# Six MLP tiles of the third token block moved to the two stretches around the last block's output projection

## The reference

```python
h = modulate(rmsnorm(x, norm_mix_w[l]), shift_a, scale_a)
proj = (h @ w_in[l]).astype(f32)
mixed = token_mix(proj, ...)          # 4 retention heads and 4 gated DeltaNet heads
x = x + gate_a[:, None, :] * (mixed @ w_out[l])
h = modulate(rmsnorm(x, norm_mlp_w[l]), shift_m, scale_m)
x = x + gate_m[:, None, :] * (jnp.square(jax.nn.relu(h @ w_ff1[l])) @ w_ff2[l])
...
return rmsnorm(x, norm_final_w)
```

## Time and profile before

| What | us |
|---|---|
| median of 3 runs | 3048.26 |
| the profiled execution, whole time | 3046.6 |
| its span in the trace | 3044.8 |
| last FF2 tile of unit 15 ends, first OUT matmul starts | 2603.85, 2617.13 |
| last OUT matmul ends, FF1 of block 3 starts | 2662.2, 2674.42 |

### The profile page before, as it was taken

One profiled execution on the slowest core, in us unless ns is written; L12 is line 12 of the kernel. 1 busy time (PEld: TensorE's weight loads), 2 busy tenths in 40 slices (PEclk: granted clock), 3 DMA queues, 4 the chain that ended last, 5 costly groups with the idle time before them and its releaser, 6 DMA issues.

```text
span 3044.8 us, 37926 instructions
## 1 busy us (share of the span) xinstructions
PE 2850.4 (94%) x14376; PEld 2380.5 (78%) x14376; DVE 1324.1 (43%) x1864; ACT 1172.8 (39%) x2040; POOL 1728.8 (57%) x1324
## 2 busy tenths in 40 slices
PE   1799979999999999999999999999999999889998
PEld 1588767888888788888888788887888888668886
DVE  4555655353535335553434525545343432421123
ACT  2133443353444434353343433444333333343332
POOL 2254555575656656576555665657565655566554
PEclk9889999999999999999999999999999999999999
DMA  5521322222232323422233222422222222423332
GB/s 221 228 80 56 101 67 68 82 80 81 81 116 90 101 70 103 140 73 93 74 104 104 90 87 87 143 78 86 79 87 80 80 82 92 142 76 97 97 97 84
DMA packets 86581, 295.10 MB, mean 97 GB/s; under 512 B 10240, under 2 KB 10240, under 8 KB 82304
## 3 DMA queue, kind: packets, MB, share of 16 engines
q1 hardware_dynamic: 64944, 247.05, 25.6%
q10 hardware_dynamic: 21456, 45.62, 4.5%
HBM read 276.90 MB, written 15.73 MB: 96 GB/s over the span
## 4 chain that ended last, share of the span: by engine, by line
PE 83%; DVE 6%; POOL 5%; issue 2%; DMA 2%; ACT 2%; SPq 0%; ACTq 0%; POOLq 0%; DVEq 0%
PE acc L392 23%; PE acc L394 22%; PE acc L393 22%; PE pm L426 7%; PE pm L431 3%; DMA mixing<-in_ada_w 2%; POOL w L1388 1%; DVE mixing L1018 1%; POOL mT L1397 1%; ACT io L636 1%; PE pm L408 1%; PE pm L545 1%; DVE x L1257 1%; PE pm L518 1%; DVE io L934 1%
## 5 line engine op out<-in xcount | busy, mean ns | idle before, releaser
L1388 POOL TENSOR_TENSOR w<-raw,w 128x512 fp32r<-128x512 f32 x832 | 1116.4, 1344 | 1047.3 <-ACT w L610 1019.1
L610 ACT ACTIVATE w<-raw 128x512 fp32r<-128x512 f32 x832 | 521.0, 627 | 783.2 <-PE acc L394 662.3
L392 PE MATMUL acc<-mT,w 128*128 128x512 f32 x1280 | 517.3, 404 | 13.0 <-POOL mT L1397 5.8
L394 PE MATMUL acc<-mT,w 128*128 128x512 f32 x1280 | 501.6, 392 | 0.0
L393 PE MATMUL acc<-mT,w 128*128 128x512 f32 x1280 | 500.4, 391 | 0.0
L392 PE MATMUL acc<-hT,w 128*128 128x512 f32 x1024 | 437.1, 427 | 41.4 <-POOL w L1388 30.8
L394 PE MATMUL acc<-hT,w 128*128 128x512 f32 x1024 | 407.8, 398 | 0.0
L393 PE MATMUL acc<-hT,w 128*128 128x512 f32 x1024 | 406.7, 397 | 0.0
L1229 DVE SCALAR_TENSOR_TENSOR x<-acc,ab,x 128x512 f32<-128x512 f32 x256 | 191.4, 750 | 450.3 <-PE acc L394 450.1
L392 PE MATMUL acc<-hid,w 128*128 128x512 f32 x896 | 364.4, 407 | 13.8 <-POOL hid L1402 8.3
L394 PE MATMUL acc<-hid,w 128*128 128x512 f32 x896 | 350.3, 391 | 0.0
(11 more groups left out here) (201 smaller groups left out, 3828.0 us busy)
## 6 DMA issues: line engine op xcount, KB each, us to landing
raw<-in_w_all SPq DMA_DIRECT2D x416, 512.0 KB, 3.6
mixing<-in_ada_w SPq DMA_DIRECT2D x24, 1024.0 KB, 7.3
xr<-in_xT ACTq DMA_DIRECT2D x48, 256.0 KB, 2.9
out<-io ACTq DMA_DIRECT2D x32, 256.0 KB, 2.6
mixed_kept<-mixing ACTq DMA_DIRECT2D x28, 256.0 KB, 2.0
xr<-mixed_kept ACTq DMA_DIRECT2D x28, 256.0 KB, 2.7
x<-in_xT ACTq DMA_DIRECT2D x6, 1024.0 KB, 7.3
x<-in_xT SPq DMA_DIRECT2D x1, 2048.0 KB, 17.4
```

Source lines behind the costliest of these rows:

```text
L392: e.matmul(bank, whi, x[:, 0, :], start=first, stop=False)
L394: m = e.matmul(bank, wlo, x[:, 0, :], start=False, stop=last)
L610: e.activation(w2[:, 0, local % HALVES, :], raw[:, tile % NRAW, local % 2 * NT:(local % 2 + 1) * NT], ACT.Copy).then_inc(S["w_hi"], 1)
L1388: e.tensor_tensor(w2[:, 1, local % HALVES, :], raw[:, tile % NRAW, local % 2 * NT:(local % 2 + 1) * NT], w2[:, 0, local % HALVES, :].bitca ...
```

## The change

`dense_plan` moves six tiles and adds none. Of the 24 tiles of unit 15, the last six of block 2's MLP are held back: FF2 tiles 2 and 3 of group 6, and all four FF2 tiles of group 7. The first two stand in slots 0 to 7 of stretch 16 (2 k-steps a slot), the other four in slots 30 to 39 (3 a slot, 5 in the last). Unit 15 keeps 18 tiles: 5 k-steps in each two slots up to slot 51, 1 a slot in slots 52 to 61, 2 in the last two. In it FF1 of groups 6 and 7 now stand in a row, before FF2 of group 6.

Since block 2's residual is now complete only at slot 39, block 3 gets its own, `x1_late`, over `mixing` next to `hid_late`. ACT issues its load at slot 47 of unit 15. The hidden tile of group 7 of block 2 is kept in `hT`, free by then. The final norm of block 2 moves from slots 1 to 9 to slots 41 to 50: its squares (line 629) and their sums (929), which stood beside the readouts of group 7, now stand in slots 41 and 42 as a block, and column sums, power, diagonal, row, output tiles and output DMAs in slots 44 to 50.

```diff
             new += list(two[NG - 2]) + list(two[NG - 1])
-            per = [0] * 8 + [3] * 21 + [1] + [0] * 10 + [22] * 23 + [6]
+            held = ff(b - 2, NG - 2)[1][2:4] + ff(b - 2, NG - 1)[1]
+            new = held[0:2] + new[0:KT] + held[2:6] + new[KT:]
+            per = [2] * 8 + [3] * 21 + [1] + [3] * 9 + [5] + [22] * 23 + [6]
         elif u == 0:
             o = [(OUT, b - 1, j, 0) for j in range(KT)]
...
-                new = a5 + c5 + a6 + c6 + a7 + c7
-                per = [3] * SLOTS
-        assert sum(per) == KT * len(new), n
+                new = a5 + c5 + a6 + a7 + c6[0:2]
+                per = [3, 2] * 26 + [1] * 10 + [2] * 2
+        assert sum(per) == KT * len(new) and len(per) == SLOTS, n
...
+        last_residual = nc.sbuf_tensor("x1_late", [P, KT, NT], F32)
+        x1_late = last_residual.__enter__()
         late_hidden = nc.sbuf_tensor("hid_late", [P, 2, FFG, NT], F32R)
         hid_late = late_hidden.__enter__()
         late_hidden.__exit__(None, None, None)
+        last_residual.__exit__(None, None, None)
         mixing = sb("mixing", [P, 16, NT])
...
         def hidden(b, g):
+            if b == NB - 2 and g == NG - 1:
+                return hT[:, :, 0:FFG, :]
             return hid_late if b == NB - 1 and g % 2 else hid
+
+        def residual(b):
+            return x1_late if b == NB - 1 else x1
 
...
-                        if s == 3:
+                        if s == (44 if n == UNITS else 3):
                             column_sums(NORM["f", b - 2], bC)
-                        if s == 5:
+                        if s == (46 if n == UNITS else 5):
                             row_everywhere(NORM["f", b - 2], bC)
...
                 elif i == 0 and b == NB - 1 and g == 0:
-                    e.wait_ge(S["w_used"], used((FF2, b - 1, NG - 1, FFG - 1)))
+                    e.wait_ge(S["w_used"], used((FF2, b - 1, NG - 2, FFG - 1)))
+                elif i == 0 and b == NB - 2 and g == NG - 1:
+                    e.wait_ge(S["w_used"], used((PROJ, UNITS - 1, UNIT - 1, 0)))
                 elif i == 0 and b < NB - 1 and (b or g):
...
-                    square(NORM["m", b], i, x1[:, i, :])
-                if k % 4 == 3 and kind == FF2 and i == NG - 1:
+                    square(NORM["m", b], i, residual(b)[:, i, :])
+                if k % 4 == 3 and kind == FF2 and i == NG - 1 and b != NB - 2:
                     o = 2 * y + k // 4
                     e.wait_ge(S["ff2_evac"], 2 * NG * FFG * b + 2 * FFG * i + o + 1)
-                    square(NORM["f", b], o, x1[:, o, :])
...
+                    if n == UNITS and s in (41, 42):
+                        if s == 41:
+                            e.wait_ge(S["ff2_evac"], 2 * NG * FFG * (NB - 1))
+                        for j in range(4 * (s - 41), 4 * (s - 40)):
+                            square(NORM["f", b - 2], j, x1[:, j, :])
+                    put = s - 41 if n == UNITS else s
+                    if u == 0 and b >= 2 and put in (7, 8, 9):
+                        for j in {7: (0, 1, 2, 3), 8: (4, 5), 9: (6, 7)}[put]:
                             e.wait_ge(S["o_ready"], KT * (b - 2) + j + 1)
                             e.dma_start(out[b - 2, :, j, :], io[:, j % 4, :]).then_inc(OSEM[j % 4], 16)
-                            if j == 3:
+                            if j == 3 and n < UNITS:
                                 e.dma_start(x1[:, 0:4, :], xT[b - 1, :, 0:4, :]).then_inc(S["x1_lo_in"], 16)
-                            if j == 7:
+                            if j == 7 and n < UNITS:
                                 e.dma_start(x1[:, 4:8, :], xT[b - 1, :, 4:8, :]).then_inc(S["x1_hi_in"], 16)
+                    if n == UNITS - 1 and s == 47:
+                        e.wait_ge(S["y_out"], (LEVELS - 1) * UNITS)
+                        e.wait_ge(S["u_next"], UNITS)
+                        e.wait_ge(S["mr_kept"], 16 * UNITS)
+                        e.dma_start(x1_late[:, 0:4, :], xT[NB - 1, :, 0:4, :]).then_inc(S["x1_lo_in"], 16)
+                        e.dma_start(x1_late[:, 4:8, :], xT[NB - 1, :, 4:8, :]).then_inc(S["x1_hi_in"], 16)
                     if u == 0 and b >= 1 and 36 <= s <= 39:
                         for j in (2 * (s - 36), 2 * (s - 36) + 1):
...
+                    if n == UNITS and 41 <= s < 43:
+                        for j in range(max(1, 4 * (s - 41)), 4 * (s - 40)):
+                            add_square(NORM["f", b - 2], j)
                     if u == 0 and b >= 2:
                         f = NORM["f", b - 2]
-                        if s == 1:
+                        at = s - 41 if n == UNITS else s
+                        if at == 1 and n < UNITS:
                             add_square(f, KT - 1)
-                        if s == 3:
+                        if at == 3:
                             scaled_sums(f, bC)
-                        if s == 4:
+                        if at == 4:
                             diagonal(f)
-                        if s == 5:
+                        if at == 5:
                             keep_row(f, bC)
-                        if s in (6, 7):
-                            for j in (0, 1) if s == 6 else (2, 3):
+                        if at in (6, 7):
+                            for j in (0, 1) if at == 6 else (2, 3):
                                 out_tile(b - 2, j)
                     if n < UNITS:
                         mix(n, s)
...
-                    if u == 0 and b >= 2 and s == 4:
+                    if u == 0 and b >= 2 and s == (45 if n == UNITS else 4):
                         rms_power(NORM["f", b - 2])
```

23 lines of the change are left out of this document (11 added, 12 removed).

## The result

The changed kernel takes **3026.5 us** (median of 4 runs, 3025.48 to 3031.15). The kernel before took 3048.99 beside it (4 runs, 3047.57 to 3050.59). The ratio is 0.9935, with a 95% interval of 0.9923 to 0.9946. Forecast were 3024.9, with a range of 3018.9 to 3034. The profiled execution took 3025.81, its span is 3024.0, 20.8 less than before.

A forecast was written before the change was run, and what follows sets the result against it. PE, busy 94% of the span, bounds the kernel; only its waits and half clock can be won. Gains 12.3 + 11.9 + 2.7, less 0.5, 1.0 and 2.0, give 23.4: 3048.26 to 3024.9 us, range 3018.9 to 3034.

The forecast's parts named there:

- First stretch: Slots 0 to 7, before OUT: two held tiles cover the tail and the final norm leaves; gain 12.3 us.
- so the transpose in slot 7 waits for nothing: Slot 7: the tail with a readout ahead and one inside takes 7.5 us, against 10.9 of held tiles.
- Second stretch: Slots 30 to 39, OUT to FF1: four held tiles cover the norm; gain 11.9 us, less 0.5 for clock.
- The bound on the other side: Slots 30 to 39: all 8 high and low halves lengthen the chain by 15.8; gain 6.0 instead of 11.9.
- Rival 1: FF1 after slots 30 to 39: PE waits for low parts, POOL being shared with weights; 3030.3 us; rivals 1 to 3 together 0.29.
- Unit 15: Unit 15: two of three waits for the hidden tile gone, gain 2.7 us; thinning costs 1.0.
- rival 2: Thinned end of unit 15: the recurrence bounds it, costing 5.5 instead of 1.0; 3029.4 us; rivals 1 to 3 together 0.29.
- Final norm in the MLP: Slots 41 to 50: the norm among MLP tiles costs 2.0 us, ends 0.5 and 6.2; narrow place slot 42.
- The upper end of 6.2: Slot 42: each of DVE's four adds held for a whole POOL instruction of 1.30; total 3029.1 us.
- Rival 3: OUT: the stall only moves, loads and weights come late, first stretch brings half (6.1); 3031.0 us; rivals 1 to 3 together 0.29.
- Rival 4: Slots 30 to 50: the woven norm stalls PE up to seven times, 6.6 us each; 3068 us, slower; chance 0.04.
- Rival 5: Whole kernel: nothing measurable, the end moves by under 6 us, four stalls cost 26.4; 3048 us; chance 0.05.

The follow-up runs named there:

- thin: The changed kernel with unit 15 thinned further: 3 k-steps a slot to slot 41, 1 in slots 42 to 59, none in 60 to 63; 3030.55 us.
- two held: The changed kernel with only the first stretch filled, by two FF2 tiles of group 7; unit 15 keeps 22 tiles; 3033.32 us.
- the second run of after: The changed kernel, unaltered, measured once more; 3027.72 us.
- no hidden wait: The changed kernel with FF1 of group 6 also ahead of FF2 of group 5, hidden tiles of groups 6 and 7 sharing `hT`; 3021.96 us.
- square on ACT: The changed kernel with one four-element product moved from DVE to ACT as a square, in all 16 units; 3026.05 us.
- four held: The changed kernel with only the second stretch filled, by all four FF2 tiles of group 7; unit 15 keeps 20 tiles; 3035.8 us.
- adds early: The changed kernel with squares and adds of block 2's final norm one slot earlier, in slots 40 and 41; 3024.15 us.
- norm early: The changed kernel with block 3's MLP norm three slots earlier in stretch 16; 3023.34 us.
- no held tiles: The changed kernel with its buffer and late final norm, but all 24 tiles back in unit 15 in the old order; 3046.66 us.

## Why the prediction was right, and where its steps were off

**First stretch: 12.3 forecast, 11.4 measured.** The tail with the readout ahead of it took 8.05 us for 7.5. It held one readout inside, as was assumed, but the sum had no term for POOL, whose instructions held it up by some 1.7. The step "so the transpose in slot 7 waits for nothing" is true by its words and missed the wait: it looked at the transpose, and not at the readout that stands behind the tail on DVE. PE waits 0.73 us for that one. In other kernels it is 0.7 to 3.3.

**Second stretch: 11.9 less 0.5 forecast, 11.7 measured,** or 11.0 with the 0.7 us of half clock that reach into the second FF1 tile. The eighth k-step of FF1 started 31.8 us behind OUT's end, where 32.2 were worked out. That is near by some luck, since the sum is not what its text says: it adds 1.3 and 0.7, where the two high halves and the one low half that it names come to 2.6. The bound on the other side does not follow either: 15.8 in place of those 2.0 would leave no gain at all (1.9 lost), not one of 6.0. The waits for the low parts were 0.25, 0.22, 1.51 and 0.18, together 2.2 instead of some 3.5:

```profile
2653.34 0.47 PE L402 MATMUL acc<-mT,w 128*128 128x512 f32 x1 [0.25 <-POOL mT L1425]
...
2656.98 0.50 PE L402 MATMUL acc<-mT,w 128*128 128x512 f32 x1 [1.51 <-POOL mT L1425]
...
2658.23 0.79 PE L402 MATMUL acc<-mT,w 128*128 128x512 f32 x1 [0.18 <-POOL mT L1425]
2658.82 0.63 PE L403 MATMUL acc<-mT,w 128*128 128x512 f32 x1
```

The clock fell once behind them, as was allowed for. Rival 1 fell: it wanted 6.0 here. The crowding costs these 2.2 us and the half clock, and the norm three slots ahead took most of them away (one wait of 0.62 is left, and one of 0.47 in the held tiles).

**Unit 15: 2.7 less 1.0 forecast, 0.7 measured.** The sum is near by two errors. The recurrence cost nothing (1.0 assumed; 0.62 in the thinner kernel), so that rival 2 falls and the earlier trace rows were no measure for a unit without a next one. The gain of 2.7 shrank, since the third wait grew by 0.26 us and eight matmuls at the half clock (1.6 us) came behind it. The step that took "two of three waits gone" as their sum left out that the third one stands in a thinner unit: the half tiles on both sides of it changed.

**Final norm in the MLP: 2.0 forecast, 2.9 measured** beyond its own work. The place and the chain were right: the add began 2.6 us behind the last FF1 sum, where 2.7 were worked out. The four adds took 4.03 us; the text had 2.7 alone and 5.0 beside POOL. The wait was 2.08, in the forecast 1.0 to 3.3, and with what it delays 2.35. The other 0.7 are the half clock that comes from the second stretch, so the term itself was off by 0.35. One of the four adds was held for nearly all of a POOL instruction (1.64 us), as the forecast says of an add that begins right behind its start; the others began while POOL was idle, from 2702.39 to 2704.99. The upper end of 6.2 wanted four such holds; that it did not come says nothing against the mechanism behind it.

**Sum.** 11.4 + 11.7 + 0.7 - 2.9 = 20.9, against 23.4 forecast. The medians differ by 22.5, only 0.9 from the forecast, and that closeness is partly luck. In the two traces unit 15 began at 2438.7 in both, so there the stretch is all of the difference. The 1.6 between 22.5 and 20.9 is how far the two profiled executions lie from their medians, 2.4 under it before and 0.7 under it after; where the other executions lose the time no trace shows. Rivals 3, 4 and 5 are answered by the waits of after: OUT stands for nothing, the woven norm has one wait of 2.08 and not seven of 6.6, and without the tiles the gain is gone.

**Of the signs that were named**, PE at column sums and row without a wait and at a granted clock of 1.00, one wait in unit 15, and the wait of 1 to 3 us at the first FF2 came out. OUT started 12.3 us behind unit 15's last k-step, for "some 11"; the waits for low parts were 2.2 us for 3.5; and unit 15 was 33.3 us shorter, for 33. What the list lacked is the half clock behind a short wait in unit 15, and the readout in the first stretch.

## What to carry to other kernels

Dense tiles that depend on nothing in a serial chain can fill the time in which PE stands for it. They are worth the idle time that they cover and not their own (here 32.7 us of tiles were moved for a gain of 20.9), and only if each instruction that they and the chain put off on the engines in order, readouts above all, still comes before PE needs its bank. A wait of 2 us can cost nearly double by the clock behind it: here removing the last wait of its kind gained 3.9 us, and removing the first two, without half clock, 3.2. Where the code ahead of a change scatters by more than the effect, compare the stretch from the first changed matmul to the last.

## What the runs showed of the hardware

**DVE can be shut out by POOL for more than one instruction.** The product of 4 elements takes 0.155 us. At the end of unit 15, beside POOL instructions, it took 0.31 to 1.18 in six traces, each to the end of the POOL instruction in which it began, and 3.38 and 3.40 in two, past two such ends until POOL had a pause. The next product of the tail was held past two ends once elsewhere, for 3.71. These three are the only such cases in the fourteen traces; over 700 other small instructions of DVE that were held ended within 0.06 us of the end of a POOL instruction, and none of them took longer than 1.36 us. The Trainium skill ("SBUF — State Buffer", Who interferes with whom) says that a DVE instruction with two inputs in SBUF contends with a GpSimd instruction that reads SBUF, and that the later one blocks until the other is done. The short cases agree; by that rule the first two long ones should have ended at the first boundary, 0.9 us after their start, and the third after 1.2, and they did not. Why DVE gets in at one end and not at another stays open. It is not the moment at which the product begins: that was some 0.13, 0.18, 0.40 and 0.59 us into the POOL instruction in thin, two held, the second run of after and no hidden wait (short), and some 0.11 and 0.47 in the long ones.

**One input in SBUF does not exempt a small instruction.** L1205 of square on ACT, a TENSOR_SCALAR on one input of 4 elements, took 1.22 us to the end of the POOL instruction beside it, against 0.17 alone. The same section exempts one SBUF input outside the 2-port modes and lists tensor_scalar among those that can enter them; the row agrees only if it did so here, which no run shows.

**The half clock behind a short wait.** A wait of 2.00 or 2.01 us at the same place in unit 15 was followed by seven or eight matmuls at the 1.2 GHz level in five traces (after twice, four held, adds early, norm early) and not in square on ACT, also at 2.01. Behind waits of 1.40, 1.74 and 1.75 us there it never came. In the first stretch the last wait before OUT was 1.83 us in adds early, without it, and 1.84 in norm early, with seven such matmuls. Behind the wait of 2.08 at block 3's first FF2, which nine traces have, it came in one (no held tiles). So a wait of about 2 us may or may not cost double.
